# Loading x, grid and context tile by tile, and adding the squares of two tiles before the first norm's sums

## What is computed

```python
x = x + grid_sincos(rows, x.shape[-1])[None]
for l in range(DEPTH):
    mx = split(silu(c) @ w_ada[l] + b_ada[l], 6)
    mc = split(silu(c_ctx) @ w_ada[l] + b_ada[l], 6)
    hx = modulate(rmsnorm(x, g_pre_mix[l]), mx[0], mx[1])     # x * rsqrt(mean(x*x) + eps) * g * (1 + scale) + shift
    hc = modulate(rmsnorm(ctx, g_pre_mix[l]), mc[0], mc[1])
    out_x, out_c = token_mixers(hx, hc, w_in[l], ...)
    ...
```

## Time and profile before

| | us |
|---|---|
| median of 3 runs | 3576.95 (3576.43 to 3578.74) |
| the profiled execution, its own time | 3576.69 |
| its span, first to last instruction | 3574.9 |
| PE busy in the span | 3236.3 |

### The profile page before, as it was taken

The page is one execution under the profiler, slowest core; times in us unless marked ns, Lnnn a source line. Parts: engine busy times, 40 slices in busy tenths (PEclk is TensorE's granted clock), DMA queues, the critical chain, the costliest instruction groups (busy, mean ns, idle before and its releaser), DMA issues.

```text
span 3574.9 us, 40795 instructions
## 1 busy us (share of the span) xinstructions
PE 3236.3 (91%) x16640; PEld 2526.4 (71%) x16640; DVE 1374.9 (38%) x2570; ACT 1060.7 (30%) x1660; POOL 962.5 (27%) x476
## 2 busy tenths in 40 slices
PE   5989789999999889778999999998899899987898
PEld 4778668888888768667777766765567676755666
DVE  1575442522323454435311347333430356232512
ACT  2213432312212322433322322344322222343222
POOL 0122113222223212132444322221125232211134
PEclk9999878999999789888999899998899799998999
DMA  5233241111111123312222221111112121111121
GB/s 193 95 122 114 107 159 54 59 65 63 62 65 59 61 90 134 124 42 92 95 94 90 71 73 59 64 54 47 36 54 88 60 77 48 65 53 42 36 71 65
DMA packets 78506, 277.30 MB, mean 78 GB/s; under 512 B 8416, under 2 KB 10080, under 8 KB 78192
## 3 DMA queue, kind: packets, MB, share of 16 engines
q1 hardware_dynamic: 74736, 267.86, 21.9%
q10 hardware_dynamic: 3584, 6.84, 0.5%
HBM read 272.57 MB, written 2.10 MB: 77 GB/s over the span
## 4 chain that ended last, share of the span: by engine, by line
PE 81%; DVE 10%; ACT 5%; issue 2%; DMA 1%; POOL 1%; ACTq 0%; DVEq 0%; SPq 0%; POOLq 0%
PE pb L992 18%; PE pb L994 17%; PE pb L993 17%; PE pb L1035 4%; PE pb L1103 3%; PE pb L1403 2%; PE pb L941 2%; PE pb L1014 2%; PE pb L1015 1%; PE pb L1016 1%; PE pb L1375 1%; PE pb L1061 1%; PE pb L1361 1%; PE pb L1111 1%; DVE AR L1624 1%
## 5 line engine op out<-in xcount | busy, mean ns | idle before, releaser
L2485 POOL TENSOR_TENSOR RGR<-RG,WHI 128x1024 fp32r<-128x1024 f32 x330 | 792.0, 2401 | 2122.5 <-ACT WHI L2097 2122.5
L2097 ACT ACTIVATE WHI<-RG 128x1024 fp32r<-128x1024 f32 x330 | 345.2, 1046 | 374.0 <-PE pb L994 285.1
L992 PE MATMUL pb<-HI,WHI 128*128 128x512 f32 (+1 forms) x880 | 388.4, 441 | 19.5 <-DVE MOD L1479 6.5
L994 PE MATMUL pb<-LO,WHI 128*128 128x512 f32 (+1 forms) x880 | 358.7, 408 | 0.0
L993 PE MATMUL pb<-HI,RGR 128*128 128x512 f32 (+1 forms) x880 | 357.9, 407 | 0.0
L992 PE MATMUL pb<-HR,WHI 128*128 128x512 f32 (+1 forms) x768 | 278.9, 363 | 16.7 <-POOL RGR L2485 10.1
L994 PE MATMUL pb<-HR,WHI 128*128 128x512 f32 (+1 forms) x768 | 277.5, 361 | 0.0
L993 PE MATMUL pb<-HR,RGR 128*128 128x512 f32 (+1 forms) x768 | 277.3, 361 | 0.0
L992 PE MATMUL pb<-HIDR,WHI 128*128 128x512 f32 (+1 forms) x768 | 273.9, 357 | 1.1 <-ACT RLT L2239 0.8
L994 PE MATMUL pb<-HIDR,WHI 128*128 128x512 f32 (+1 forms) x768 | 274.8, 358 | 0.0
L993 PE MATMUL pb<-HIDR,RGR 128*128 128x512 f32 (+1 forms) x768 | 274.1, 357 | 0.0
(11 more groups left out here) (380 smaller groups left out, 5748.5 us busy)
## 6 DMA issues: line engine op xcount, KB each, us to landing
RG<-in_W_dram SPq DMA_DIRECT2D x504, 512.0 KB, 3.3
XCX<-in_xT_dram ACTq DMA_DIRECT2D x1, 2048.0 KB, 21.5
GRID<-in_grid_dram ACTq DMA_DIRECT2D x1, 2048.0 KB, 27.3
out_dram<-XCX SPq DMA_DIRECT2D x8, 256.0 KB, 2.0
CS<-in_CST_dram ACTq DMA_DIRECT2D x1, 1027.0 KB, 4.9
XCC<-in_ctxT_dram ACTq DMA_DIRECT2D x1, 1024.0 KB, 15.1
CS<-in_CST_dram SPq DMA_DIRECT2D x1, 523.0 KB, 4.8
RG<-in_W_dram SPq DMA_DIRECT2D x2, 256.0 KB, 3.0
```

The source lines that it names most:

```text
L992: e.matmul(out, hi[:, k, :], xh, start=k == order[0], stop=False)
L994: i = e.matmul(out, hi[:, k, :], xl, start=False, stop=k == order[7])
L2097: e.activation(WHI[:, u % 2, 0:n], RG[:, s % RING, 0:n], ACT.Copy).then_inc(*up("weightsA", u))
L2485: e.tensor_tensor(RGR[:, s % RING, 0:n], RG[:, s % RING, 0:n], WHI[:, u % 2, 0:n].bitcast(F32), SUB).then_inc(*up("weightsG", u))
```

## The change

- x, grid and context are loaded by tiles: for each k one transfer of x (256 KB), one of the grid (256 KB) and one of the context (128 KB), in that order, all from ACT's queue, with a semaphore `x{k}` for each tile. ACT issues 25 transfers in place of 4 before it turns to silu.
- Each tile's squares have a place of their own (`first_square(k)`, 768 columns), so ACT no longer waits for PE to have read an older square.
- DVE adds the squares of tile k-1 to those of an odd tile k (one addition of 128x768), and PE sums each pair with six matmuls (`xpair`), four times in place of eight.
- The order of steps is written out: tiles 0 and 1, piece, pair 0, piece; tiles 2 and 3, piece, pair 1; tiles 4 and 5, piece, pair 2, piece; tiles 6 and 7, piece, pair 3, piece, piece. The steps of the two tiles stand ahead of the first piece of their group.
- Nothing behind `rstd` differs in instructions or in their order.

```diff
--- before.py
+++ after.py
@@ -652,10 +652,13 @@
 def schedule():
     o = Order()
     o.step("start")
-    sums = o.begin([("xsum", k) for k in range(8)], 5.0)
-    o.adas(0, range(0, 16, 2), "w_ada", 0)
+    for pair, js in enumerate(((0, 2), (4,), (6, 8), (10, 12, 14))):
+        o.step("xsum", 2 * pair)
+        o.step("xsum", 2 * pair + 1)
+        o.adas(0, js[0:1], "w_ada", 0)
+        o.step("xpair", pair)
+        o.adas(0, js[1:], "w_ada", 0)
     o.flush()
-    o.end(sums)
     for l in range(2):
         first_layer(o, l)
     for l in range(2):
@@ -859,6 +862,9 @@
     def squares_at(tag, i):
         base = 6144 if tag == "x1a" or tag == "x2a" else norms[tag][0]
         return ar(base + NT * (1 + i % 2), NT)
+
+    def first_square(k):
+        return ar(norms["x0a"][0] + NT * k, NT)
 
     def stream_square(tag, k, g0, gn):
 
@@ -1165,9 +1171,13 @@
                     i.then_inc(*up("turnP", n))
                     pb7["last"] = ("evacA", ("turned", n))
 
-        def xsum(k):
-            for t0, tn, _ in both:
-                sum_square("x0a", t0, tn, k)
+        def xpair(pair):
+
+            e.wait_ge(*at("normV", ("first pair", pair)))
+            squares = first_square(2 * pair + 1)
+            for c in range(6):
+                m = e.matmul(sum_at("x0a", c), squares[:, c * 128:c * 128 + 128], ones[:, 0:1], start=pair == 0 and c == 0, stop=pair == 3 and c == 5)
+            m.then_inc(*up("normP", ("sums", "x0a")))
 
         def residual(tag, k):
             if following[tag]:
@@ -1498,9 +1508,11 @@
                 e.tensor_tensor(d, d, raw, ADD).then_inc(*up("evacV", ("roped", n)))
 
         def xsum(k):
-            if k == 0:
-                e.wait_ge(*at("x", "all"))
+            e.wait_ge(*at(f"x{k}", "all"))
             e.tensor_tensor(XCX[:, k, :], XCX[:, k, :], GRID[:, k, :], ADD).then_inc(*up("normV", ("grid", k)))
+            if k % 2:
+                e.wait_ge(*at("normA", ("first square", k)))
+                e.tensor_tensor(first_square(k), first_square(k), first_square(k - 1), ADD).then_inc(*up("normV", ("first pair", k // 2)))
 
         def gains(l, which):
             e.wait_ge(*at("evacV", o.last["ada", l, 0 if which == (0,) else 2]))
@@ -2077,9 +2089,11 @@
 
         def start():
             e.dma_start(VC[:, :], dram["VEC"]).then_inc(*up("vectors", "c in", by=16))
-            e.dma_start(XCC[:, :, :], dram["ctxT"].rearrange("(k p) t -> p k t", p=128)).then_inc(*up("x", by=16))
-            e.dma_start(XCX[:, :, :], dram["xT"].rearrange("(k p) t -> p k t", p=128)).then_inc(*up("x", by=16))
-            e.dma_start(GRID[:, :, :], dram["grid"].rearrange("(k p) t -> p k t", p=128)).then_inc(*up("x", "all", by=16))
+            for k in range(8):
+                rows = slice(k * 128, k * 128 + 128)
+                e.dma_start(XCX[:, k, :], dram["xT"][rows, :]).then_inc(*up(f"x{k}", by=16))
+                e.dma_start(GRID[:, k, :], dram["grid"][rows, :]).then_inc(*up(f"x{k}", by=16))
+                e.dma_start(XCC[:, k, :], dram["ctxT"][rows, :]).then_inc(*up(f"x{k}", "all", by=16))
             e.wait_ge(*at("startV", "zeros"))
             e.wait_ge(*at("vectors", "c in"))
             for i, name in enumerate(("c_2", "c", "c_ctx")):
@@ -2112,12 +2126,11 @@
             e.activation(stream_square(tag, k, g0, gn), x, ACT.Square).then_inc(*up("normA", ("squares", tag, k, g0)))
 
         def xsum(k):
-            if k == 0:
-                e.wait_ge(*at("x", "all"))
+            e.wait_ge(*at(f"x{k}", "all"))
             for t0, tn, _ in both:
                 if t0:
                     e.wait_ge(*at("normV", ("grid", k)))
-                square(xc(k, t0, tn), "x0a")
+                e.activation(first_square(k)[:, t0:t0 + tn], xc(k, t0, tn), ACT.Square).then_inc(*up("normA", ("first square", k)))
 
         def rstd(tag):
             e.wait_ge(*at("normP", ("sums", tag)))
```

More of the change, by code:

```diff
@@ L1442, in gNorm @@
             head_factors(h, GRS).then_inc(*up("glaP", ("norm", l, h)))
-        stages = {"mm": mm, "post": post, "xsum": xsum, "rstd": rstd, "residual": residual, "mPrep": mPrep, "mA": mA, "mB": mB, "mC": mC, "mD": mD, "mO": mO,
+        stages = {"mm": mm, "post": post, "xpair": xpair, "rstd": rstd, "residual": residual, "mPrep": mPrep, "mA": mA, "mB": mB, "mC": mC, "mD": mD, "mO": mO,
                   "ret": ret, "rSq": rSq, "rNorm": rNorm, "idx": idx, "head": head, "gDecay": gDecay, "gLevel": gLevel, "gOut": gOut, "gState": gState,
```

## The result

| | before | after |
|---|---|---|
| median, us | 3577.84 (3576.43 to 3581.32, 4 runs) | 3558.93 (3555.76 to 3561.78, 4 runs) |
| ratio, 95% interval | | 0.9942 (0.9929 to 0.9956) |
| profiled execution, its own time and span, us | 3576.69, 3574.9 | 3555.76, 3553.9 |
| broadcast of the first root begins, us | 77.83 | 56.22 |
| PE busy, us | 3236.3 | 3222.9 |

The medians differ by 18.9 us, the two profiled executions by 20.9, the broadcasts by 21.6. The forecast was 3553.6 with 3546 to 3561 around it.

A forecast was written before the change was run, and what follows sets the result against it. PE carried 81% of the chain, its start held by the grid load until 29.63 us. T of 15.0 plus 39.6 put the broadcast at 54.6 in place of 77.83, 23.2 us earlier: 3553.6 us, range 3546 to 3561.

The forecast's parts named there:

- T: At the start, the moment ACT's queue is through its loads; forecast 15.0 us, between 12.7 and 16.3.
- if 2450 again may be outstanding: On ACT's load queue: about 2450 packets may stay queued, so ACT is free when 1150 are done, T = 16.0.
- Rival 1: ACT's queue holds only about 1400 outstanding packets: T = 20, broadcast 59.6, time 3558.7 us; chance 15%.
- extra packets: In ACT's load queue: 16 more packets for each transfer, 3600 in all; leaving them out gives T = 14.0.
- T + 39.6: Start of the root's broadcast: 9.9 us from T to the second piece's end, then 29.7 us, giving 54.6.
- sums of a pair, on PE: Six matmuls summing a pair's squares on PE: 2.85 us (1.01 + 1.87, less a handover).
- three waits for a bank: Third, sixth and eighth pieces wait on PE for DVE's bias addition to free their bank: 0.7 us in all.
- pairs 1 and 3 wait: PE waits for DVE's pair addition at pairs 1 and 3: 0.4 us each, together 0.8 us.
- end: Last turned row, bias, gains, reciprocal, up to the broadcast: 0.6 us.
- Nothing behind differs: After the root's broadcast nothing gains or loses time (0 us), so the span changes by what the broadcast does.
- rival 2: Granted clock moves with the earlier start, 10 us either way, 3544 to 3564; chance 20%, half on either side.
- Rival 3: On ACT's queue small loads go one by one: T = 50, broadcast 89.6, slower at 3588.7 us; chance 3%.

The follow-up runs named there:

- e7_act_in_order: Changed kernel, but ACT issues constants, six weight slabs and all 24 tile loads in order of need, SP starting with the seventh slab; 3565.26 us (one run).
- e5_sp_in_order: Changed kernel with the 24 tile loads issued from SP's queue between the slabs in order of need, ACT issuing VC alone; 3548.70 us, ratio 0.9908.
- e3_loads_of_two: Changed kernel with two tiles in each load, 13 transfers in place of 25; 3553.10 us (one run).
- e2_whole_loads: Changed kernel with the three whole loads of the kernel before on one semaphore, new order and pair additions kept; 3572.04 us, ratio 0.9973.
- e6_one_sum: Kernel with tile loads on SP's queue, but DVE adds the squares of all eight tiles and PE sums once; 3550.66 us, ratio 0.9921.
- e4_no_pair: Changed kernel without DVE's pair additions, PE summing both tiles with 12 matmuls a pair; 3564.64 us, ratio 0.9961.
- e5_again: Same kernel as e5_sp_in_order, rerun on another chip against the kernel before; 3549.65 us, ratio 0.9921.

## Why the prediction was right, and where not

**What bounds the kernel.** Right: only the start moved. In the table the gains of the versions with four runs or more lie within 3.5 us of what their broadcasts gained; of the two single runs one is 7 above and one 9 below. Data held nothing, as forecast: DVE could add the grid to tile 1 at 16.57 us, ahead of T.

**When ACT is free: the term that was mis-sized.** T, the moment at which ACT's queue is through its loads, was forecast at 15.0, between 12.7 and 16.3, and is 18.31, outside its bounds. The step that failed is "if 2450 again may be outstanding". That depth was read from one blocked issue, the grid's. The DMA queues of the changed kernel from 0 to 7.33 us, when the hold begins:

```profile
q1 hardware_dynamic: 362, 1.36, 54.0%
q10 hardware_dynamic: 325, 0.59, 21.9%
```

and from 0 to 18.31, T:

```profile
q1 hardware_dynamic: 1008, 3.68, 53.5%
q10 hardware_dynamic: 1658, 2.63, 39.3%
```

At 7.33 us 12 transfers (1728 packets) had been taken from ACT and 325 moved: 1403 outstanding. At 8.82, 10.53 and 12.21 it is 1430, 1429 and 1447 in the same way, each ahead of a held issue; at 13.17 it is 1527, ahead of a short one, and at 13.65 it is 1633, ahead of a held one; at 14.69, with issues short again, 1695, and at 18.31, 1942. Rival 1 put "about 1400" outstanding, and that is what four of the six held issues show. But it is no constant: rival 1 then had ACT wait until all but 1400 were moved, T = 20, and from 14.7 us on the queue took more. The hold in the changed kernel ends with SP's six slabs (SP had moved 938 of 1008 packets by 14.69). e7_act_in_order shows a hold with SP quiet, e5_sp_in_order none on SP with 1834 outstanding. What sets the hold of ACT's queue stays open. The prediction's lower value, 14.0 without the extra packets, doesn't come out of its own terms either: some 750 packets of 1.5 KB and 3.7 MB at 399 GB/s give 14.3. The "extra packets" were right: ACT's queue moves 3600 in all, 16 more for each transfer.

So T lies between the forecast's and rival 1's, 3.3 above the one and 1.7 below the other, and the result, 3558.93, looks like rival 1's 3558.7. That is a coincidence: the broadcast is at 56.2, between 54.6 and 59.6, and the other 2.7 us were lost behind it, where rival 1 has nothing.

**The rounds.** Forecast T + 39.6, measured T + 37.9 in the changed kernel (56.22 - 18.31), in e3_loads_of_two (55.87 - 17.95) and in e7_act_in_order (57.58 - 19.66). By its terms:

| step | forecast | measured |
|---|---|---|
| first square behind T | 2.0 | 1.9 |
| four squares | 2.1 | 1.7 |
| pair addition | 0.92 | 0.96 |
| sums of a pair, on PE | 2.85 | 2.65 |
| three waits for a bank | 0.7 | 0.8 |
| pairs 1 and 3 wait | 0.8 | 0.4 |
| end | 0.6 | 0.6 |

The sums were the second term that was mis-sized, because two rows of a chain (1.01 + 1.87) were added: each holds an end that overlaps the next matmuls. The distance between the start of the sums and of the piece behind them (22.99 and 25.64) is what a group costs PE. This applies four times, 0.8 us; the squares, 0.4, and the pair waits, 0.4, make up nearly all of the rest of the 1.7.

**What follows the broadcast.** "Nothing behind differs" is right in the order, and wrong by some microseconds in time. By the profiled executions 23.2 was forecast and 21.6 came at the broadcast (3.3 lost at T, 1.7 won back), 21.8 at the last root, 20.9 in the time. The medians, 18.9 and 18.3 on two chips, are 3 us below that. The windows show that two executions of the changed kernel are 5 us apart after the first 600 us, with the same instructions and another granted clock in parts of them, so the profiled execution was a lucky one; it is also the fastest of its four runs.

The eleven traces of this case show how single executions fall. The stretch between the two roots near 600 us takes 27.44 or 27.45 us in six of them, 26.90 to 26.94 in four, and 25.16 in this one alone. From the broadcast to the end of the span it is 3497.1 us before (broadcast at 77.83), 3506.1 in e2_whole_loads (66.42), 3505.9 in e7_act_in_order (57.58), 3497.7 and 3503.1 in the two executions of the changed kernel, 3495.4 in e3_loads_of_two (55.87) and 3494.8 in e6_one_sum (47.58). That is 11 us of spread which doesn't go with the place of the broadcast, and it is what puts e3_loads_of_two 7 us above and e7_act_in_order 9 below their broadcasts. That e4_no_pair loses only 3.9 us for a broadcast 8.7 later, and e5_again wins 11.1 for one 8.1 earlier, on the same chip, is of the same size. Whether a shift of the start changes the clock on average (rival 2), four or five runs of a kernel don't tell; both comparisons of the changed kernel lie 3 us short, and a cause for that is not shown. Rival 2's 10 us either way is not seen between medians.

**Rival 3** fell: all 25 transfers, 3600 packets, were through by 28 us, so they overlap. In the changed kernel the DMA engines move 406 GB/s from 4 to 14 us, where before it was 399:

```profile
4.00:14.00 10.00, 0.00 (x0) 0.00 (x0) 0.69 (x1) 0.00 (x0) 0.00 (x0) 1.00 1.03 406
```

With it goes what the Trainium skill would have cost the change ("DMA: Bandwidth & Descriptors", section "Bandwidth"), which has the rule to batch to 1 MiB or more. The figures that the page gives for it, and its 2.0 us for one transfer, were taken with transfers issued from GpSimd; those here come from ACT and SP. In this case, with many transfers queued and SP's slabs of 512 KB beside them, loads of 128 and 256 KB left the DMA engines as busy as those of 1 and 2 MB. What small transfers cost here is another thing, the time of the engine that issues them.

**The range.** 3546 to 3561 holds the median and not every execution (3561.78 is one), for the reason just named. The forecast's own bounds, 3550 to 3556, did not hold it: they were bounds of T and of one addition, and had nothing for the spread of executions.

## What to carry to other kernels

Here a load issued from ACT's queue cost ACT 0.45 to 0.6 us even when nothing blocked, and more when it was held: count issues times that as work of the engine, and give loads to an engine that has nothing else to do, in the order in which they are wanted (the broadcast came 8 to 9 us earlier by it, more than a third of what the whole change brought). Where a queue's depth enters a sum, one blocked issue gives no constant; keep the range open to the side of a later start. The cost of a group of small matmuls is the distance from its start to the start of what follows, not the sum of the chain's rows.

## What was unexpected of the hardware

- Issues of ACT were held at 1403 to 1447 and at 1633 outstanding packets in the changed kernel, at 1405 to 1800 in e3_loads_of_two, and at 746 and 1721 in e7_act_in_order. They were not held at 1891, where the last issue of the changed kernel begins, or at 1463 in the middle of e7_act_in_order (3024 taken and 1561 moved at 12.0 us); SP's was not held at 1834.
- Two executions of one kernel with the same start come apart by 5 us, a part of it at a granted clock of 0.60 against 0.57 between the same two roots, where PE is busy for 23.42 of 25.16 us and for 24.76 of 26.91: by 1.8 us there, and by 3.2 before.
